# A state-space mixer turned feature-major: cumulated logs broadcast by DMA, diagonal blocks masked on GpSimd, group means by a product with ones

## The reference

```python
def mamba2_ssd(z, xbc, dt_raw, conv_w, conv_b, dt_bias, a_log, d_skip, norm_w):
    xbc = silu(causal_depthwise_conv(xbc, conv_w, conv_b))
    xs, bm, cm = split_cols(xbc, [B_WIDTH, G * N, G * N])      # 512, 2*128, 2*128
    dt = softplus(dt_raw + dt_bias)                             # one per frame and head, 8 heads
    a = dt * (-exp(a_log))
    ...
    y_diag = einsum("bcgls,bcgrls,bcsgrp->bclgrp", cb, l_mat, xdt)
    ...
    y = y_diag + y_off + x * d_skip
    y = y.reshape(b, L, B_WIDTH) * silu(z)
    yg = y.reshape(b, L, G, B_WIDTH // G)                       # 2 groups of 256 features
    yg = yg * rsqrt(mean(yg * yg, axis=-1, keepdims=True) + B_NORM_EPS)
    return yg.reshape(b, L, B_WIDTH) * norm_w
```

## Time and profile before

| What | us |
|---|---|
| median of 3 executions (2634.49 to 2646.68) | 2636.67 |
| the profiled execution, its own time | 2641.89 |
| the span of that execution in the trace | 2639.9 |
| PE busy in the span | 2382.5 |
| VectorE busy | 1208.2 |
| ScalarE busy | 908.4 |
| GpSimd busy | 104.1 |
| attention's last product ends, last row before the stage | 228.19 |
| first product of out_proj | 321.65 |

### The profile page before, as it was taken

How to read it: one execution, slowest core, us unless ns; L and a number is a source line. 1 busy time by engine, 2 the same in 40 slices (tenths; PEclk the granted TensorE clock), 3 DMA queues, 4 the chain that set the end, 5 groups by cost and what they waited for, 6 DMA issues and landing times.

```text
span 2639.9 us, 41692 instructions
## 1 busy us (share of the span) xinstructions
PE 2382.5 (90%) x17177; PEld 2104.3 (80%) x17177; DVE 1208.2 (46%) x1623; ACT 908.4 (34%) x1189; POOL 104.1 (4%) x169
## 2 busy tenths in 40 slices
PE   6989889999989777777949999999999999999995
PEld 5965788888878666645848989898989999999995
DVE  3264443323244576635247888888878300000001
ACT  3344232222132233225206667666666200000001
POOL 6000000000000000000000010101010100000000
PEclk9998599999999888898959999999999999999998
DMA  6310023342222000010049999999999977877663
GB/s 190 105 32 1 32 64 96 96 132 87 89 80 76 17 2 2 2 48 17 1 146 330 348 335 345 334 347 332 347 325 328 299 255 240 276 253 250 231 224 109
DMA packets 333823, 450.34 MB, mean 171 GB/s; under 512 B 8335, under 2 KB 291830, under 8 KB 333646
## 3 DMA queue, kind: packets, MB, share of 16 engines
q1 hardware_dynamic: 328926, 433.66, 48.9%
q0 software_dynamic: 4720, 14.00, 2.2%
HBM read 435.13 MB, written 12.51 MB: 170 GB/s over the span
## 4 chain that ended last, share of the span: by engine, by line
PE 85%; DVE 7%; ACT 4%; issue 2%; DMA 1%; DVEq 0%; SPq 0%; POOLq 0%; ACTq 0%; POOL 0%
PE bank L660 81%; PE bank L663 4%; DVE arena L1739 2%; DVE slot L1739 1%; DVE w_low L1739 1%; ACT w_high L1660 1%; DVE arena L1766 0%; ACT arena L1469 0%; DVE small L1788 0%; ACT arena L1366 0%; DMA xs<-in_x_dram 0%; ACT slot L1478 0%; DMA arena<-h_rows_d,idx_ahead 0%; DMA xs<-sum_rows_d 0%; DMA sum_rows_d<-arena,idx_now 0%
## 5 line engine op out<-in xcount | busy, mean ns | idle before, releaser
L1739 DVE TENSOR_TENSOR w_low<-slot,w_high 128x2048 fp32r<-128x2048 f32 x172 | 393.5, 2291 | 317.9 <-ACT w_high L1345 269.6
L660 PE MATMUL bank<-arena 128*128 128x144 f32 (+8 forms) x2768 | 383.1, 306 | 4.5 <-ACT arena L1413 2.6
L660 PEld LDWEIGHTS bank<-arena 128*128 128x128 f32 (+3 forms) x2768 | 343.1, 193 | 20.3 <-issue 11.3
L660 PE MATMUL bank<-w_high,xg_high 128*128 128x256 f32 x1120 | 324.6, 290 | 10.8 <-DVE w_low L1739 6.5
L660 PE MATMUL bank<-w_low,xg_high 128*128 128x256 f32 x1120 | 317.7, 284 | 3.0 <-issue 3.0
L660 PE MATMUL bank<-w_high,xg_low 128*128 128x256 f32 x1120 | 316.6, 283 | 0.0
L660 PE MATMUL bank<-arena,slot 128*128 128x144 f32 (+3 forms) x2304 | 298.8, 312 | 19.3 <-ACT slot L1582 14.8
L660 PEld LDWEIGHTS bank<-arena,slot 128*128 128x128 f32 (+2 forms) x2304 | 284.8, 193 | 30.2 <-ACT slot L1582 15.9
L1739 DVE TENSOR_TENSOR arena<-arena,bank 128x256 f32<-128x256 f32 (+3 forms) x134 | 63.9, 477 | 528.6 <-PE bank L660 528.6
L1739 DVE TENSOR_TENSOR w_low<-arena,w_high 128x2048 fp32r<-128x2048 f32 x105 | 240.6, 2291 | 56.6 <-ACT w_high L1660 56.6
L660 PE MATMUL bank<-h_high,w_high 128*128 128x512 f32 x592 | 235.9, 398 | 6.8 <-DVE h_low L1739 6.8
(11 more groups left out here) (354 smaller groups left out, 3388.9 us busy)
## 6 DMA issues: line engine op xcount, KB each, us to landing
slot<-in_moe_w_gate_dram SPq DMA_DIRECT2D x64, 1024.0 KB, 6.1
arena<-in_moe_w_down_dram SPq DMA_DIRECT2D x64, 1024.0 KB, 5.7
slot<-in_moe_w_up_dram SPq DMA_DIRECT2D x56, 1024.0 KB, 6.7
arena<-in_moe_w_up_dram SPq DMA_DIRECT2D x56, 1024.0 KB, 6.7
arena<-in_moe_w_gate_dram SPq DMA_DIRECT2D x48, 1024.0 KB, 5.6
slot<-in_moe_w_down_dram SPq DMA_DIRECT2D x48, 1024.0 KB, 6.6
slot<-in_e_w_in_dram SPq DMA_DIRECT2D x12, 1024.0 KB, 5.4
slot<-in_ff_w_gate_dram SPq DMA_DIRECT2D x11, 1024.0 KB, 5.4
```

The lines of the kernel that those rows point to most:

```text
L660: return pe.matmul(o, lhsT, rhs, start=start, stop=True, skip_group_check=True)
L1739: return dve.tensor_tensor(o, a, b, op)
```

## The change

Everything behind the products of a head becomes feature-major, and what PE did to build the decay rows moves to other engines:

- z is projected by feature (4 tiles of 512 columns where there were 8 of 256) and silu(z) is kept as zsT.
- cum is written to DRAM and read back broadcast to 128 partitions for all heads at once (`cum_b`, 2 MB in SBUF), both on SP's queue ahead of the load of ("e_out", 1); the broadcast waits for the convolution (`conv_sum`), whose input lies in that region.
- dt_col is made before attention. GpSimd forms, for each head, the four diagonal blocks cum[l] - cum[s] by an add of a broadcast column and puts the mask in by an affine select (`seg_d`, three buffers).
- ScalarE takes exp of the diagonal blocks (one instruction) and of the three plain parts straight into wT (three buffers), and copies cbT out of PSUM; VectorE multiplies wT by cbT in place.
- PE's product of a head has xdt (64 columns) as weights and wT moving, four products (512, 384, 256, 128 columns) into one half of a bank.
- The gate is done for pairs of heads (`gated`), the squares on ScalarE, the group mean by a product of `ones` with the squares (`y_sums`), the inverse root on a full 128x512 tile (`group_scale`), and the norm on feature-major tiles (`normed`). `x_tok` is no longer stored; the transposes back go away. `out_proj` waits for all parts at once.

```diff
+                if item == ("e_out", 1):
+                    sp.wait_ge(sem("cum_ready"), 1)
+                    sp.dma_start(cum_d[0].rearrange("(h l) -> h l", l=SEQ), dt_row[1]).then_inc(sem("cum_moved"), 16)
+                    sp.wait_ge(sem("cum_moved"), 16)
+                    sp.wait_ge(sem("conv_sum"), CONV_TILES)
+                    sp.dma_start(cum_b.rearrange("p h l -> p (h l)"), cum_d[0:1, :].to_broadcast([P, HEADS * SEQ])).then_inc(sem("cum_moved"), 16)
...
+            pool.wait_ge(sem("dt_col_ready"), 1)
+            pool.wait_ge(sem("cum_moved"), 32)
+            for h in range(HEADS):
+                if h >= 3:
+                    pool.wait_ge(sem("decay_ready"), NT * (h - 3) + 1)
+                link(pool.tensor_tensor(seg, cum_b[:, h, :].rearrange("p (j l) -> p j l", l=P), from_col, ALU.add))
+                pool.affine_select(out=seg, in_=seg, compare_op=ALU.is_ge, fill=MASKED, base=0, pattern=[[0, NT], [1, P]],
+                                   channel_multiplier=-1).then_inc(sem("seg_masked"), 1)
...
-                            m = mm(b[:, :], head_row[:, h, :], dt_row[1], True)
-                                    m = mm(b[:, P * j:P * (j + 1)], ident[:, :], causal_mask[:, :], False)
-                                m = mm(b[:, HD * l:HD * (l + 1)], wT[g % 2][:, j, P * l:P * (l + 1)],
-                                       xdt[:, j, HD * g:HD * (g + 1)], l == 0)
+                def y_sums(g):
+                    b, former = tile("ssd_ms_ready", g + 1)
+                    pe.wait_ge(*former)
+                    for i in range(2):
+                        pe.wait_ge(sem("y_squared"), 2 * g + i + 1)
+                        m = mm(b[:, :], ones[:, :], y_squares[:, 2 * g + i, :], i == 0)
+                    m.then_inc(sem("ynT_full"), 1)
+                pe.wait_ge(sem("x_tok_ready"), NT)
+                for h in range(HEADS):
+                    if h % 2 == 0 and h >= 4:
+                        pe.wait_ge(sem("y_tok_ready"), h // 2 - 1)
+                    if h == 6:
+                        y_sums(0)
+                    rows = slice(HD * (h % 2), HD * (h % 2) + HD)
+                    for j in range(NT):
+                        pe.wait_ge(sem("w_ready"), NT * h + j + 1)
+                        m = mm(acc[h // 2 % 2][rows, P * j:], xdt[:, j, HD * h:HD * (h + 1)], wT[h % 3][:, j, P * j:], j == 0)
+                    m.then_inc(sem("ssd_full"), 1)
+                y_sums(1)
-                out_proj(0, [y_high_even[:, k, :] for k in range(KT)], [EVEN_PARTS + 4 + t + 1 for t in range(NT)])
+                out_proj(0, [y_high_even[:, k, :] for k in range(KT)], [EVEN_PARTS + KT] * NT)
...
                 for h in range(HEADS):
+                    if h >= 3:
+                        act.wait_ge(sem("ssd_full"), h - 2)
+                    act.wait_ge(sem("seg_masked"), h + 1)
+                    act.activation(diag_w[h % 3], seg_d[:, h % 3, :, :], ACT.Exp).then_inc(sem("decay_ready"), 1)
+                    for j in range(NT - 1):
+                        act.activation(wT[h % 3][:, j, P * (j + 1):], cum_b[:, h, P * (j + 1):], ACT.Exp,
+                                       bias=small[:, 64 + HEADS * j + h:65 + HEADS * j + h]).then_inc(sem("decay_ready"), 1)
+                    if h < B_GROUPS:
+                        for i in range(NT * h, NT * h + NT):
+                            j = i % NT
+                            act.wait_ge(sem("cb_full"), i + 1)
+                            act.activation(cbT[:, h, j, P * j:], bank["cb_ready", i + 1][:, P * j:], ACT.Copy).then_inc(sem("cb_ready"), 1)
+                    if h == 5:
+                        for p in range(2):
+                            y_square(p)
...
+                def gated(p):
+                    dve.wait_ge(sem("ssd_full"), 2 * p + 2)
+                    dve.wait_ge(sem("z_stored"), 4)
+                    step(dve.scalar_tensor_tensor(out=yT[:, 4 + p, :], in0=conv_out[:, p, :], scalar=small[:, 8 + p:9 + p], in1=acc[p % 2][:, :],
+                                                  op0=ALU.mult, op1=ALU.add))
+                    tt(yT[:, 4 + p, :], yT[:, 4 + p, :], zsT[:, p, :], ALU.mult).then_inc(sem("y_tok_ready"), 1)
+                def group_scale(g):
+                    dve.wait_ge(sem("ynT_full"), g + 1)
+                    step(dve.tensor_scalar(y_scale[:, g, :], bank["ssd_ms_ready", g + 1][:, :], 1.0 / 256, B_NORM_EPS, ALU.mult, ALU.add))
+                    dve.reciprocal(y_scale[:, g, :], y_scale[:, g, :]).then_inc(sem("ssd_ms_ready"), 1)
...
+                group_scale(0)
+                normed(0)
+                gated(3)
+                group_scale(1)
+                normed(1)
                 out_proj(E_OUT, 0, 0)
```

More of the change, by code:

```diff
@@ L552, in _ @@
             link(pool.memset(chunk_mask[0:CHUNK, CHUNK:P], MASKED))
-            link(pool.memset(causal_mask[:, :], 0.0))
-            select(causal_mask[:, :], ALU.is_ge, MASKED, 0, [[1, P]], -1)
             link(pool.memset(ones[:, :], 1.0))
@@ L784, in _ @@
                 else:
-                    full, stored = ("v_full", "v_stored") if c < 6 else ("z_full", "z_stored")
+                    full, stored = "v_full", "v_stored"
                     for t in range(NT):
@@ L1832, in _ @@
             dve.wait_ge(sem("const_ready"), 1)
-            dve.wait_ge(sem("small_loaded"), 64)
+            dve.wait_ge(sem("small_loaded"), 80)
             for c in (6, 7):
@@ L1857, in _ @@
             if upto >= 2:
+                dve.wait_ge(sem("dt_col_full"), 1)
+                dve.tensor_copy(small[:, 64:128], bank["dt_col_ready", 1][:, 0:64]).then_inc(sem("dt_col_ready"), 1)
                 for p in range(HEADS // 2 * NT + 1):
@@ L1899, in _ @@
-                for h in range(HEADS + 1):
-                    if h == 7:
-                        gate_squares(0)
+                for k in range(4):
+                    dve.wait_ge(sem("part_high"), EVEN_PARTS + k + 1)
+                    tt(y_low[:, k, :], yT[:, k, :], y_high_even[:, k, :].bitcast(F32), ALU.subtract).then_inc(sem("part_low"), 1)
+                    dve.wait_ge(sem("x_tok_full"), k + 1)
+                    dtc = small[:, 96 + HEADS * k:96 + HEADS * (k + 1)].unsqueeze(2).to_broadcast([P, HEADS, HD])
+                    tt(xdt[:, k, :].rearrange("p (h n) -> p h n", n=HD), bank["x_tok_ready", k + 1][:, :].rearrange("p (h n) -> p h n", n=HD), dtc,
+                       ALU.mult).then_inc(sem("x_tok_ready"), 1)
@@ new lines, in _ @@
+                for h in range(HEADS):
+                    if h in (3, 5):
+                        gated(h // 2 - 1)
+                    if h == 7:
+                        gated(2)
+                    for j in range(NT):
+                        if h % 4 == 0:
+                            dve.wait_ge(sem("cb_ready"), h + j + 1)
+                        dve.wait_ge(sem("decay_ready"), NT * h + min(j + 2, NT))
+                        tt(wT[h % 3][:, j, P * j:], wT[h % 3][:, j, P * j:], cbT[:, h // 4, j, P * j:], ALU.mult).then_inc(sem("w_ready"), 1)
```

180 lines of the change are left out of this document (56 added, 124 removed).

## The result

The changed kernel takes 2612.2 us (median of 4 executions, 2610.8 to 2617.8), the kernel before, measured beside it, 2636.5 (2634.5 to 2646.7, 4 executions). The ratio is 0.9895, interval 0.9876 to 0.9914: 24 us less, where 31 were forecast. In the profiled executions it is 2617.76 against 2641.89.

What follows compares the result with a forecast made beforehand. PE at half clock was taken to pace mixer B's heads. With VectorE pacing, start, loop and tail put `out_proj` at 285.8, 35.9 us earlier; less 2, 1 and 2, gain 31: 2605.5 us, range 2596 to 2621.

Steps and rivals of the forecast that it cites:

- Attention and before: Ahead of the stage: dt_col and z cost nothing, under 1 us if uncovered; cum broadcast there by 196, 38 us to spare.
- GpSimd's part: Masked diagonal blocks: add 1.5 and select 0.63, 2.1 us a head; three heads done by 203, the rest hidden.
- The start: From y's upper half to VectorE's first head: first cbT copy done at 237.0, first head at 244.0, 5 us later than before.
- The loop: The eight heads: VectorE sets the pace with 22.3 us if PE's clock is up, ending at 266.3.
- The tail: Behind the loop: group 0 7.7 us, last pair 11.8, each with a 3.4 us reciprocal; `out_proj` at 285.8.
- rival E: The tail's reciprocals cost no more than a copy, 2 x 2.8 us less, 2600 us; chance 0.10.
- Set aside: Taken off the gain: 2 us for `out_proj` starting at the lower clock, 1 for signals, 2 for GpSimd beside VectorE.
- Rival C: Full exclusion of VectorE by GpSimd, 13 us lost instead of 2, gain 20, 2617 us; chance 0.13.
- Rival B: PE stays at half clock in the heads, 4.3 us a head, `out_proj` at 295, gain 23.5, 2613 us; chance 0.20.
- D: GpSimd is the bound and the change slower, needing 13.3 us a head to meet the old 321.65; chance 0.03.

Runs made afterwards that it cites:

- e4: The changed kernel with ScalarE's Ln and Exp making the inverse root, in place of VectorE's scale and reciprocal and ScalarE's root; 2605.7 us, ratio 0.9862.
- e3: The changed kernel with the row broadcasts and mask products put back on PE, 48 products more into banks nobody reads; 2626.4 us.
- e5: The changed kernel with 48 small unread products more in PE's program, in its wait behind attention; 2623.5 us, ratio 0.9935.
- e12: The fastest kernel until then (2587.1 us) with 48 unread 8 x 8 products more in PE's waits ahead of the expert loops; 2582.7 us, ratio 0.9779.
- e2: The changed kernel with a head's product in its old shape, ten products moving 64 columns, output misplaced so only the stage is compared; 2692.4 us.
- e9: The changed kernel with GpSimd's first three heads' masked differences held back until attention's twelfth scaled tile; 2614.6 us, ratio 0.9901.
- e7: The changed kernel with Ln and Exp replacing the reciprocals, x's transposes and products earlier, and ScalarE's weight halves behind head 2; 2599.3 us, ratio 0.9843.
- e1: The changed kernel with GpSimd doing only a one-column operation for heads 3 to 7, their masked blocks left out; 2612.9 us.

## Why the prediction came out as it did

Right: that VectorE would pace the loop with PE's clock up, hence a gain, and the measured 2612.2 lies in the range. The gain was forecast 7 us too large. By the prediction's own steps:

- **Attention and before.** dt_col and the broadcast show no cost of their own: SP issued the broadcast at 175.36, GpSimd began on it at 182.75, 13 us sooner than "by 196". Attention's last products began 1.7 us later than before, which I can't tell from the spread of 5 us between profiles.
- **GpSimd's part.** 1.05 for an add, not 1.5; 0.63 for a select, as worked out. The pair is 1.7, and up to 2.8 beside VectorE (1.89 and 0.90). Three heads were done by 188.4.
- **The start.** The first cbT copy ended at 238.4 against 237.0, attention's 1.7 explaining it; VectorE's first head was at 246.6 against 244.0. The 1.2 in between are mostly one y_low of 1.48 (0.68 alone), ahead of the last x tile: the lock, and an instruction that I hadn't counted in that place.
- **The loop.** 23.2 against 22.3. Without the lock it would be 21.4. The clock came back during group 1's cbT (3.11 us, 3.2 forecast) and was 1.00 from 244 to 268.
- **The tail.** 7.5 for group 0 (7.7 forecast), 12.1 for the last pair (11.8 forecast, though its parts add up to 11.7). The reciprocal, trusted least, was 3.35 against 3.4: a slope over eight columns held to 512 (156 ns and 511 times 6.6 would be 3.5). e4, with no reciprocal, shows what rival E's world would have been worth.
- **Set aside.** `out_proj` began at 289.4, 3.6 us behind the sum's 285.8. The 3 us set aside for GpSimd and signals nearly cover that, but in part by luck: 1.7 of the 3.6 are attention's later end, 0.9 the start, 0.9 the loop and 0.1 the tail. 2 us were set aside for its start at the lower clock: "to FFN" lost 1.7 against "to out_proj". At that mark the gain was 30.4, forecast 31.
- **The step that failed** is one that the prediction never wrote down: that behind `out_proj` everything only shifts. PE's program got shorter by some 300 products, PE waits twice where it waited once at the change of the expert loops, and 5.5 us were given back there, 1900 us later. That it hangs on the number of products ahead of the loop is shown (e3, e5, e12); that a block border of PE's instructions moved is how I read it. The rest, 1 us, is in the scatter.

Rival C had 13 us lost to GpSimd. The runs show 1.8 in the loop and 0.8 at the start, for two reasons: the loss is 0.6 us per recorded us and not 1, and only the last two of the five pairs that were left lay beside VectorE's loop, the three before them being done when it began at 246.61. Rival B's lower clock comes with the old shape (e2), and with the new one for three heads in some executions (e5, e9). D was far off: 1.7 us a head against the 13.3 at which it would decide.

## What to carry to other kernels

When the engine that is 90% busy runs at the lower clock, look at the shape of its products as well as at its amount of work: here turning one product round, so that 512 columns move instead of 64, took the heads from 0.50 to 1.00 (e2 against the change). By itself that was worth 5.6 us of the stage, and taking the broadcasts and masks off PE 18, where the whole change gave 34. Follow a gain down the program by landmarks, for it can be given back where nothing was changed; a wait of PE that nothing in the profile explains, at a change of loops, is worth trying with a few dozen hidden products. Work started earlier on GpSimd or VectorE may only move into each other's way: 10 us of an earlier start gave 6.5.

## What the runs showed of the hardware

- An fp32 reciprocal on VectorE costs 6.5 ns per column (3.35 us for 512), five times a copy's rate, and both of this kernel's were on the path (e4).
- VectorE's products with two SBUF inputs lose 0.6 us per us of GpSimd's adds and selects beside them (1.8 for 3.1 in the change; 5.1 for 8.1 in e7's 21 products). GpSimd's own slow down as well: adds 1.05 to 1.48 and 1.89, selects 0.63 to 0.90. Even a one-column instruction of GpSimd took 1.04 us beside VectorE, and 0.20 elsewhere (e1).
- A product of 8 columns costs 0.2 us with a load of 128 columns (e5), but 0.03 with a load of 8 columns (e12: 64 in 1.76 us), both at a clock of 0.50.
- PE waited 4.4 to 5.3 us at a change of loops, a packet of the instruction queue moving in each wait, once or twice by the number of products ahead in its program.
- With PE busy without a gap and 64 columns moving, the granted clock fell to 0.50 and stayed there for 22 us (e2). With up to 512 columns moving and weights of 64 columns it was 1.00, but in two profiles 0.50 for some 6 us (e5, e9).
